# Neighbourhood attention by grid column, and two small stages folded into their neighbours

## The reference, cut to what matters

```python
x = first_block(...)                    # ends with: return rms_norm(x, final_norm_g)
z = rmsnorm(h, mix_norm) @ mix_w_in     # second block, i = 0; h = x
...                                     # RWKV on part of z, a long convolution on the rest, FFN, embedding
z = rmsnorm(h, na_norm) @ na_w_qkv      # i = 1
h = h + neighbourhood_attention(z, ...) @ na_w_out

def neighbourhood_attention(z, q_g, k_g, rpb):      # 16 heads of 64, kh = 8 rows, kw = 16 columns
    q = split(rmsnorm(q, q_g) * (dh ** -0.5)); k = split(rmsnorm(k, k_g)); v = split(v)
    cstart = np.clip(col - kw // 2, 0, GRID_W - kw)
    col_idx = cstart[:, None] + np.arange(kw)[None, :]
    def row_block(i):                   # all 8 grid rows are in every window
        s = einsum('bhqd,bhrqwd->bhqrw', q_i, k_win) + rpb[:, dr_idx][:, :, dc_idx]
        pr = softmax(s over (kh, kw))
        return einsum('bhqrw,bhrqwd->bhqd', pr, v_win)
```

## Time and profile before

| | us |
|---|---|
| median of 3 runs (4033.49 to 4035.83) | 4035.28 |
| the profiled execution | 4031.27 |
| its span on the core | 4029.5 |

### The profile page before, as it was taken

How to read it: one execution, slowest core, us unless ns; L and a number is a source line. 1 busy time by engine, 2 the same in 40 slices (tenths; PEclk the granted TensorE clock), 3 DMA queues, 4 the chain that set the end, 5 groups by cost and what they waited for, 6 DMA issues and landing times. The chain is left out here.

```text
span 4029.5 us, 54251 instructions
## 1 busy us (share of the span) xinstructions
PE 3475.5 (86%) x22936; PEld 2332.5 (58%) x22936; DVE 1964.2 (49%) x2913; ACT 1113.2 (28%) x1843; POOL 310.2 (8%) x248
## 2 busy tenths in 40 slices
PE   7689799998778979999695667759999998799998
PEld 6377543333637653333383556627888785368887
DVE  3654432323366432322446565565664542967645
ACT  3343300001254310000222221123333421653333
POOL 1010000000001000000102232200000100300000
PEclk9899899999889989999896788879999997999999
DMA  5022279998102139999420000011222221412221
GB/s 197 11 90 78 86 319 427 427 428 369 69 27 105 61 119 428 428 427 428 178 101 23 2 2 3 3 39 68 105 97 81 94 98 40 64 68 105 103 75 73
DMA packets 78840, 599.29 MB, mean 149 GB/s; under 512 B 35124, under 2 KB 37428, under 8 KB 43336
## 3 DMA queue, kind: packets, MB, share of 16 engines
q1 hardware_dynamic: 78600, 595.84, 37.4%
HBM read 593.72 MB, written 2.10 MB: 148 GB/s over the span
## 5 line engine op out<-in xcount | busy, mean ns | idle before, releaser
L574 PE MATMUL psum<-source_hi,weights_hi 128*128 128x512 f32 (+1 forms) x2352 | 923.7, 393 | 104.7 <-DVE weights_lo L486 81.1
L574 PE MATMUL psum<-source_lo,weights_hi 128*128 128x512 f32 (+1 forms) x2352 | 914.2, 389 | 0.0
L574 PE MATMUL psum<-source_hi,weights_lo 128*128 128x512 f32 (+1 forms) x2352 | 913.0, 388 | 0.0
L574 PEld LDWEIGHTS psum<-source_hi,weights_hi 128*128 128x128 f32 x2352 | 449.4, 191 | 206.4 <-DVE weights_lo L486 95.8
L574 PEld LDWEIGHTS psum<-source_lo,weights_hi 128*128 128x128 f32 x2352 | 450.2, 191 | 89.8 <-issue 2.4
L574 PEld LDWEIGHTS psum<-source_hi,weights_lo 128*128 128x128 f32 x2352 | 449.9, 191 | 89.5
L1476 PE MATMUL psum<-weight_ring_first,branches 128*64 128x512 f32 x2048 | 465.6, 597 | 17.1 <-DMA weight_ring_first<-in_w_up 8.7
L486 DVE TENSOR_TENSOR weights_lo<-weight_ring_second,weights_hi 128x1024 fp32r<-128x1024 f32 (+3 forms) x230 | 285.1, 1244 | 301.0 <-ACT weights_hi L441 300.8
L1476 PEld LDWEIGHTS psum<-weight_ring_first,branches 128*64 128x64 f32 x2048 | 138.1, 137 | 305.3 <-issue 271.9
L441 ACT CAST weights_hi<-weight_ring_second 128x1024 fp32r<-128x1024 f32 (+3 forms) x230 | 228.3, 997 | 266.8 <-PE psum L574 248.9
L1627 DVE TENSOR_TENSOR x<-psum,x 128x512 f32<-128x512 f32 x256 | 164.1, 685 | 203.7 <-PE psum L1509 203.7
(11 more groups left out here) (363 smaller groups left out, 4530.5 us busy)
## 6 DMA issues: line engine op xcount, KB each, us to landing
weight_ring_first<-in_w_gate SPq DMA_DIRECT2D x64, 2048.0 KB, 17.7
weight_ring_first<-in_w_up SPq DMA_DIRECT2D x64, 2048.0 KB, 19.3
lent_weights<-in_w_down SPq DMA_DIRECT2D x64, 2048.0 KB, 18.4
weight_ring_second<-in_ffn_w_up SPq DMA_DIRECT2D x22, 2048.0 KB, 7.9
weight_ring_first<-in_xattn_w_kv SPq DMA_DIRECT2D x8, 2048.0 KB, 8.0
weight_ring_second<-in_ffn_w_down SPq DMA_DIRECT2D x8, 2048.0 KB, 8.0
weight_ring_first<-in_w_in SPq DMA_DIRECT2D x6, 2048.0 KB, 24.4
weight_ring_second<-in_mix_w_in SPq DMA_DIRECT2D x6, 2048.0 KB, 8.1
```

What stands on the lines that cost most here:

```text
L574: ins = pe.matmul(ps, a, b, start=k == 0 and q == 0, stop=k == job.rows // P - 1 and q == 2)
```

## The change

It has three parts.

1. The norm stage between the blocks is gone. The chain `split_in` splits `x` itself, with the product of both gains (`final_gain`); its own norm takes squares weighted with the first gain (`final_weight`), and a second norm (`final`) rescales `x` in place for the residual, after all source tiles are split. The two columns of products are made in the first block, by GpSimd and by a square root of ScalarE, in both layers.
2. The stage that loads the RWKV tables is gone. The DMAs stand at the head of `split_in`'s SyncE queue, the mask is made in `rwkv_low_rank`.
3. Tokens of queries, keys and values are stored by grid column (`c r` in place of `r c`), queries shifted by 8 columns. A tile of 128 queries is 16 columns, and sees only the keys of two tiles: the same and the next, or for the last tile the first and the last. A step makes 256 scores for each head in place of 512, 4 transposes in place of 8, one copy in place of two. The bias table comes from the host with its mask, 512 KB a pair in one DMA. GpSimd has nothing to do.

```diff
+            act.activation(self.square[:, q % 2, 0:norm.n_tok], norm.src(k)[:, 0:norm.n_tok], ACT.Square,
+                           scale=1.0 if norm.weight is None else norm.weight[:, k:k + 1]).then_inc(self.squared, 1)
...
             if norm.gain is not None:
+                if norm.is_source:
+                    dve.wait_ge(self.src_lo, len(self.tiles))
...
+                pool.tensor_tensor(K.final_gain, gain, K.cols("mix_norm_2", 0, KT), ALU.mult).then_inc(columns_made, 1)
+                pool.tensor_tensor(K.final_weight, gain, gain, ALU.mult).then_inc(columns_made, 1)
...
+                act.activation(K.final_weight, K.final_weight, ACT.Sqrt, bias=K.eps[:, 0:1]).then_inc(columns_made, 1)
...
-                    norm = Norm(stream(K), range(KT), 1.0 / D, spread_at=2)
+                    norm = Norm(stream(K), range(KT), 1.0 / D, spread_at=2, weight=K.final_weight, eps=3)
+                    final = Norm(stream(K), range(KT), 1.0 / D, gain=K.cols("final_norm_g", 0, KT), square_at=2, spread_at=6,
+                                 root_at=7)
+                    final.is_source = True
...
-                chain(K, split_in, "centred", "convolved")
-            rwkv(K, z, ya)
+                chain(K, split_in, "centred", "convolved", first=load_rwkv(K, arena[:, 16:20, :]))
+            rwkv(K, z, ya, arena[:, 16:20, :])
...
-        norm(K, K.x, K.x, column("final_norm_g", 0, KT))
...
+def near_attention(K, q, k, v, pairs=8):
...
+                sp.dma_start(table[:, p % 2], K.dram["na_bias"][p].rearrange("q (c a k) -> q c a k", c=2, a=2))\
+                    .then_inc((landed0, landed1)[p % 2], 16)
...
+                    tiles = k[rows(a), p, :].rearrange("p (s t) -> p s t", t=P)
+                    keys = tiles[:, qt:qt + 2, :] if qt < TT - 1 else tiles[:, 0:TT:TT - 1, :]
+                    ins = pe.matmul(K.psum[:, 2 * (j % 2) + a, 0:W], q[rows(a), p, qt * P:(qt + 1) * P], keys,
+                                    start=True, stop=True)
...
+                for qt in range(TT):
+                    for s, tile in enumerate(key_tiles(qt)):
+                        for a in range(2):
+                            ins = pe.matmul(K.psum[rows(a), 6 + p % 2, qt * P:(qt + 1) * P],
+                                            v[:, tile, (2 * p + a) * HEAD:(2 * p + a + 1) * HEAD],
+                                            probT[:, p % 2, qt, a, s, :], start=s == 0, stop=s == 1)
...
+                src = K.psum[:, 6 + p % 2, :].rearrange("p (c r) -> p c r", c=GRID_W)
+                to = by_rows(q[:, p, :])
+                dve.tensor_copy(to[:, 8:, :], src[:, 0:GRID_W - 8, :])
+                dve.tensor_copy(to[:, 0:8, :], src[:, GRID_W - 8:, :]).then_inc(out_kept, 1)
...
+                    root = by_rows(r[0])
+                    if i >= KT:
+                        return eng.tensor_tensor(cut(k[:, i - KT, :]), cut(ps), root, ALU.mult)
+                    to = cut(q[:, i, :])
+                    eng.tensor_tensor(to[:, GRID_W - 8:, :], cut(ps)[:, 0:8, :], root[:, 0:8, :], ALU.mult)
+                    return eng.tensor_tensor(to[:, 0:GRID_W - 8, :], cut(ps)[:, 8:, :], root[:, 8:, :], ALU.mult)
...
+                          view=(by_columns, lambda a: a.rearrange("p (r c) -> p r c", c=GRID_W)))
```

342 lines of the change are left out of this document (173 added, 169 removed).

## The result

The changed kernel takes 3963.45 us (median of four runs, 3959.82 to 3969.37), the kernel before in the same comparison 4035.47 (4033.49 to 4035.83). The ratio is 0.9824, with a 95% interval of 0.9807 to 0.9841: 1.8% faster. The profiled executions have spans of 4029.5 us before and 3962.9 us after, 66.6 us apart, and both have a mean granted clock of 0.927.

A forecast was written before the change was run, and what follows sets the result against it. It read bounds by stretch: norm and late weights' DMA at the border, an idle load stage, VectorE plus stalls in attention. -13.0 - 7.4 - 51.2 + 0.5 + 0.4 = -70.7 from 4031.3, plus 4.0: 3965 us, range 3949 to 3987.

The forecast's parts named there:

- Border: Norm stage between the halves goes: first matmul of the next chain 14.6 us earlier, net -13.0 us with added chain work.
- The cover of the root: In the border chain, the seventh weights are split by 35.7 us, before TensorE needs them at 35.8; cost +0.5 us.
- Columns: Queries, keys and sources stored by column: strided accesses taken as free, +0.4 us for extra instructions.
- the first rival: Strides cost something, on output copies and last source tile: 3971 us at twice, 3984 at four times; chance 0.12.
- Start of attention: One DMA a pair and no mask work: first exponential at 3423.1 against 3435.43, 12.3 us saved.
- Loop: Attention loop: steps of 1.57 us in place of 2.41 and shorter stalls, 70.7 us against 107.6, so -36.9.
- The stall: VectorE's wait behind TensorE's output product, 2.0 us in each of seven pairs, from a product of 2.35 us.
- Tail: From attention's last scaling to the next chain: 6.9 us before, 2.0 us less expected.
- Loads that don't pair: Rival: the output product's weight loads don't run side by side, stall 2.1 us longer, eight times: 3982 us; chance 0.10.
- a width that isn't half the time: Rival: half-width attention instructions don't take half the time, a step of 2.1 us: 3982 us; chance 0.06.
- a slower outcome: Rival: strides from a factor of about seven make the kernel slower than before, 4054 us at 8; chance 0.02.
- TensorE at 1.2 GHz: Rival: TensorE falls to its lower clock in the attention loop, a pair takes 14.7 us: 4012 us; chance 0.04.

The follow-up runs named there:

- loads_later: Changed kernel with the three RWKV loads issued behind the chain's first weight transfers in place of ahead of them; 3963.6 us.
- dense: Changed kernel with every stride but those of queries and keys taken out, which changes what is computed; 3954.67 us.
- after: The changed kernel itself, with all three parts of the change, against the kernel before; 3963.45 us.
- mask_left_out: Kernel before the change with GpSimd's mask addition left out, VectorE waiting for the table's DMAs instead; 4021.12 us, 0.9969 of before.
- split_output: Changed kernel with each pair's output product cut into four query tiles, one in each step; 3955.8 us.
- attention_only: Changed kernel with the new attention kept, but the old border norm stage and RWKV load stage put back; 3987.91 us, 0.989 of before.
- load_stage_back: Changed kernel with the RWKV load stage put back behind the chain and its transfers taken out of the chain's start; 3971.63 us.
- two_orders: Changed kernel with the source split twice: in order for queries and keys, by column for values; 3961.2 us.
- addition_back: Changed kernel with a GpSimd addition of the old size, on tiles nobody else uses, put back for each pair; 4000.44 us.
- strided_reads: Changed kernel with source splits reading at a step of 64 words and writing in order; 3968.05 us.

## Why the prediction was right, point by point

**The sum** came out at 3965 against 3963.45 us, closer than its terms. Against the working, the five stretches are off by +2.3, -1.2, +5.0, +1.5 and -3.5 us, 4.1 together. And the working put the median 4.0 us above the profiled execution, where it lies 0.75 below (3964.2). That the two nearly cancel is luck; that the time lies in the range is not, since the two large parts, the border and the attention stage, came as worked out.

*Border.* Predicted 14.6 us to the first matmul, measured 15.0: the issues stood 1.58 us into the stage, not 2.1, and the landing took 8.78, where 8.67 was put. The chain behind took 0.9 us more, where 1.6 was put. The cover of the root held: TensorE waited for no weights. The load stage went whole; loads_later shows that what the change put in its place costs 2.7 us, the 2.1 of issues and 0.6 of landing of the working.

*Columns: the step that failed.* "I take a stride as free, +0.4 for the extra instructions." It cost 6.3 us in the chain of the sources, shown by dense; the miss of 5 in the stretch is less because other stages in it came out shorter, the head norms by 2.6. Two things were wrong. The row with a step of two words is free indeed (the same operation takes 0.75 us dense), but it is not a price for a step of 8 or 64: those take 1.5 to 1.8 times as long. Here the page "Advanced Engine Details and Errata" of the Trainium skill, section Memory Cachelines, had the right sign: an access pattern that touches a new 16-byte line each time pays. The trace agrees, and adds the factor, 1.27 against 0.73 us on ScalarE and 1.26 against 0.75 on VectorE. And the place was wrong. The first rival counted only the last source tile, 1.35 us for each added multiple, since it took the first seven to lie beside TensorE's 5.44 us an output. The rate of 7.54 us a source shows that these tiles are links of a round over ScalarE and VectorE; each of them counts. With eight tiles in place of one, the rival would have given 0.6 to 0.75 times 10.8, some 7 us, close to the 6.3 that dense got back. Right was that the evacuations stay hidden beside TensorE's outputs.

*Start of attention.* Predicted 12.3, measured 12.5 (the first exponential 5.2 us into the stage, before 17.7).

*Loop.* 70.7 predicted, 70.5 measured: 32 steps of 1.61 (51.4; put at 50.2), seven copies of 0.88 (6.2; put at 5.0; in dense they are 0.2 us shorter each, the strides again), six stalls of 1.48 and one of 3.10 (12.0; put at 14.0) and 0.9 for the start (put at 1.5). The errors of +2.4 and -2.6 us cancel. Six kernels have this attention code, and their loops take 70.5 to 74.3 us, with a longer stall (2.2 to 3.1 us) in one to three pairs of each. After's is the shortest, so a miss of only 0.2 us is luck. The stall was mis-sized mostly because the product took 1.97 us and not 2.35: its loads do pair, 32 in 1.97 us. What matters held: with GpSimd gone, TensorE is late next (mask_left_out), by its product (split_output).

*Tail.* Put at 4.9 us, measured 6.75, since TensorE fell to the lower level at the end. Three kernels with the same code in which it didn't have 4.6 (attention_only, load_stage_back, two_orders); split_output has 3.4.

*What no term covered.* +2.8 us in the first half, -3.5 behind attention, and the 2.6 of the head norms. The extra square root takes 0.31 us and runs at 492.0 us for the first time. ScalarE's function table load just ahead of it already stood at 488.6 in place of 485.5, and between 384.0 and 426.7 the same code took 1.5 us longer at a granted clock of 0.92 in place of 0.96. So the shift was there before anything new ran. With 14 us between the shortest and longest first half of one code, and 4 us behind attention, neither needs a cause in the change. The head norms are different: 55.8 us in both kernels with the old attention, 53.1 to 53.4 in all others. That cause stays open.

**The rivals.** Strides at about 1.7: half right, see above. Loads that don't pair, a width that isn't half the time (a step of 2.1) and a slower outcome are out by the rows. TensorE at 1.2 GHz came for one pair and the tail, 3 to 4 us in all, and not for the loop; addition_back shows what it costs, 2.7 us, in a pair where it comes.

## What to carry to other kernels

Before pricing a removed wait, look for the wait behind it; the cheapest test is to leave the waiting work out, as in mask_left_out, where 22.8 us of stalls in a loop were worth 4.4. Before calling a slower instruction hidden, find which engine sets the rate in that very stretch: the same split was free beside TensorE's outputs and dear in the round ahead of them. And cut a long block of the late engine into pieces behind each step: that took 7.9 us out of the loop, though the four pieces together (0.59 us each from start to start) are longer than the block of 1.97 us.

## What the runs showed of the hardware

VectorE and GpSimd hold each other up. A VectorE instruction on two columns lasts to the end of a GpSimd addition that runs beside it (2.60 us for 0.17), even on separate data. An addition of 512 words that GpSimd starts during a VectorE source split ends 1.10 to 1.16 us after that split, whether the split is long or short (3182.66 and 3183.80 in after, 3181.08 and 3182.24 in dense, 3177.42 and 3178.52 in strided_reads), and a weights' split started during the addition ends 1.07 or 1.08 us after the addition. So the one seems to wait for the other's end, and a longer instruction on one is paid for on both. VectorE's reductions, which read PSUM, kept their 0.42 us beside an addition of 3.17 (addition_back).

A strided access costs on VectorE and ScalarE alike, for reads and for writes (f32, 512 words, steps of 8 and 64 words): 1.1 to 1.3 us in place of 0.69 to 0.75.

Equal busy shares came with different granted clocks. In the loop of after it was 1.00 at TensorE busy shares of 0.80, 0.77 and 0.80 in three stretches of 10 us, and 0.83 at 0.80 in another; in split_output it stayed at 1.00 at shares of 0.90 to 0.95. The same products took 1.97 us at the higher level (2.4 GHz) and 3.4 to 3.7 where most or all of them ran at the lower (1.2 GHz).

The same first half took 1954.0 to 1968.5 us in eleven kernels, so an edit of 2 to 5 us is read from its stretch of the trace and not from a median of four or five runs.
